# A two-block transformer kernel: query products from whole single-precision weights, embedding weights loaded ahead of the expert rows, values between single query blocks

## What is computed

```python
def _peer(h, w_q, sub_keys_1, sub_keys_2, expert_u, expert_v):
    q = (h @ w_q).reshape(B, S, PEER_HEADS, PEER_DKEY)
    s1 = jnp.einsum('bshd,nd->bshn', q[..., :half], sub_keys_1)
    s2 = jnp.einsum('bshd,nd->bshn', q[..., half:], sub_keys_2)
    v1, i1 = lax.top_k(s1, PEER_TOPK)
    v2, i2 = lax.top_k(s2, PEER_TOPK)
    cand = (v1[..., :, None] + v2[..., None, :])
    best, ci = lax.top_k(cand, PEER_TOPK)
    expert_idx = ia * PEER_NKEYS + ib
    gates = jax.nn.softmax(best, axis=-1)
    a = gelu(einsum('td,thkd->thk', hx, u)) * gx
    return einsum('thk,thkd->td', a, v)
```

## Time and profile before

| | us |
|---|---|
| median of 3 runs | 1351.69 (1349.7 to 1352.07) |
| the profiled execution | 1353.7 |
| its span, first to last instruction | 1352.0 |
| TensorE busy | 1215.2 (90%) |
| VectorE busy | 1059.7 (78%) |
| ScalarE busy | 616.0 (46%) |
| POOL busy | 290.1 (21%) |

### The profile page before, as it was taken

How to read it: one execution, slowest core, us unless ns; L and a number is a source line. 1 busy time by engine, 2 the same in 40 slices (tenths; PEclk the granted TensorE clock), 3 DMA queues, 4 the chain that set the end, 5 groups by cost and what they waited for, 6 DMA issues and landing times. The chain is left out here.

```text
span 1352.0 us, 19494 instructions
## 1 busy us (share of the span) xinstructions
PE 1215.2 (90%) x6952; PEld 908.0 (67%) x6952; DVE 1059.7 (78%) x2161; ACT 616.0 (46%) x1265; POOL 290.1 (21%) x280
## 2 busy tenths in 40 slices
PE   7999999999989877778877777787899999999998
PEld 5999999999743333324332232333699999999998
DVE  7898678887879777777766777777699978898666
ACT  4666555656333333332433333233563265554445
POOL 1010000002545544344444434443000000000000
PEclk9999999999999999999999999999999999999999
DMA  9966446665999999999999999999853545454461
GB/s 388 384 225 249 187 158 235 245 234 234 375 422 426 427 428 428 427 427 427 427 427 427 427 428 428 428 427 428 341 187 126 187 137 183 180 187 173 174 236 43
DMA packets 55488, 416.64 MB, mean 308 GB/s; under 512 B 6113, under 2 KB 6753, under 8 KB 9202
## 3 DMA queue, kind: packets, MB, share of 16 engines
q0 software_dynamic: 37152, 268.45, 47.2%
q1 hardware_dynamic: 17792, 146.51, 29.3%
q10 hardware_dynamic: 466, 0.63, 0.1%
HBM read 414.52 MB, written 1.05 MB: 307 GB/s over the span
## 5 line engine op out<-in xcount | busy, mean ns | idle before, releaser
L1109 PE MATMUL ps<-arena 128*128 128x512 f32 x512 | 234.6, 603 | 57.0 <-ACT arena L1613 57.0
L1109 PE MATMUL ps<-ring,arena 128*128 128x512 f32 x440 | 214.1, 637 | 47.1 <-ACT arena L1613 47.1
L2377 DVE CUSTOM_DVE_ANT_0 arena<-arena 128x1024 f32<-128x1024 f32 x128 | 151.7, 1223 | 99.0 <-DMA arena<-in_experts,rowid 96.3
L1109 PEld LDWEIGHTS ps<-arena 128*128 128x128 f32 x512 | 92.7, 189 | 193.9 <-ACT arena L1613 98.0
L659 POOL DMA_INDIRECT arena<-in_experts,rowid x128 | 128.7, 1005 | 351.7 <-DVE rowid L2304 191.0
L1109 PEld LDWEIGHTS ps<-ring,arena 128*128 128x128 f32 x440 | 86.1, 202 | 170.4 <-issue 92.6
L772 PE MATMUL ps<-h_hi,w_lo 128*128 128x256 f32 x700 | 194.9, 278 | 0.0
L1606 ACT ACTIVATE arena<-arena 128x2 f32<-128x2 f32 x126 | 25.6, 203 | 369.1 <-DVE arena L2377 368.9
L770 PE MATMUL ps<-h_hi,w_hi 128*128 128x256 f32 x672 | 189.0, 281 | 3.0 <-DVE w_lo L1959 2.4
L771 PE MATMUL ps<-h_lo,w_hi 128*128 128x256 f32 x672 | 187.2, 279 | 0.0
L2377 DVE CUSTOM_DVE_ANT_0 ring<-ring,arena 128x1024 f32<-128x1024 f32 x112 | 133.3, 1222 | 35.4 <-DMA ring<-in_experts,rowid 26.5
(11 more groups left out here) (424 smaller groups left out, 2558.4 us busy)
## 6 DMA issues: line engine op xcount, KB each, us to landing
ring<-in_early_w SPq DMA_DIRECT2D x43, 1024.0 KB, 5.0
arena<-in_ada_w SPq DMA_DIRECT2D x24, 1024.0 KB, 8.1
arena<-in_up_w SPq DMA_DIRECT2D x11, 2048.0 KB, 7.8
arena<-in_z_w SPq DMA_DIRECT2D x8, 2048.0 KB, 7.9
arena<-in_down_w SPq DMA_DIRECT2D x8, 1408.0 KB, 6.1
arena<-in_o_w SPq DMA_DIRECT2D x2, 2048.0 KB, 8.1
arena<-in_early_w SPq DMA_DIRECT2D x3, 1024.0 KB, 7.6
arena<-in_experts,rowid POOLq DMA_INDIRECT x128
```

The source lines that it names most:

```text
L1109: mm = pe.matmul(BK[4 + 2 * t + b], diag[:, j, :], rows[j][:, D + b * 512:D + (b + 1) * 512], start=first and j == 0, stop=last and j == ( ...
L2377: v.tensor_tensor_reduce(out=u, in0=u, in1=h2tok[:, t, :], scale=1.0, scalar=0.0, op0=ALU.mult, op1=ALU.add, accum_out=dots[:, even, j:j + ...
```

## The change

- `pq` joins `WHOLE`: query products take the chunk as loaded, and the input `x2` whole, 8 matmuls to a block. `part`, `rest`, `lo_of_x2` for them go. `low_halves` corrects a count.
- Each query chunk has one place; the ring places of rows 9 to 15 are dealt out anew. The last six chunks are loaded in the order `PQ_ORDER`, each after a product of the `wo` stage at the latest.
- `ple_w` moves to memory that `x2_hi` had; the embedding loads follow the query chunks without a wait.
- POOL: six rows at once, more after block 5, and pairs 0 to 5 of step 1 before rows 14 and 15 of step 0.
- TensorE: a value pair of step 0 behind nearly every query block.
- On ScalarE and VectorE the work of heads is reordered accordingly (dots 5 and 6 ahead of scores, weights of pairs 5 to 7 earlier).

```diff
-WHOLE = ("iq", "yb", "ya")
+WHOLE = ("iq", "pq", "yb", "ya")
 PARTED = [n for n, c in enumerate(CHUNKS) if c[0][0] not in WHOLE]
 PARTED_EARLY = len([key for key in EARLY if key[0] not in WHOLE])
 PQ = CHUNK_AT[("pq", 0)]
 BB = CHUNK_AT[("bb", 0)]
-PARTED[PARTED.index(BB):PARTED.index(PQ) + 2] = [BB, PQ, BB + 1, PQ + 1, *range(BB + 2, PQ)]
 PG = CHUNK_AT[("pg", 0)]
 
 
-PQ_HOME = {PQ: ("row", 5, 6, None, None), PQ + 1: ("row", 7, 8, None, None), PQ + 2: ("row", 2, 3, None, None),
-           PQ + 3: ("ring", 0, 5, PQ - 4, PQ - 3), PQ + 4: ("ring", 1, 6, PQ - 3, PQ - 2),
-           PQ + 5: ("ring", 2, 4, PQ - 2, PQ - 1), PQ + 6: ("ring", 3, 5, PQ - 1, PQ + 3),
-           PQ + 7: ("ring", 0, 1, PQ + 3, PQ + 4)}
+PQ_HOME = {PQ: ("row", 8, None), PQ + 1: ("row", 7, None), PQ + 2: ("row", 6, None), PQ + 3: ("ring", 5, PQ - 3),
+           PQ + 4: ("ring", 2, PQ - 2), PQ + 5: ("ring", 6, PQ - 2), PQ + 6: ("ring", 0, PQ - 4),
+           PQ + 7: ("ring", 1, PQ - 3)}
+PQ_ORDER = [PQ + 2, PQ + 6, PQ + 3, PQ + 7, PQ + 4, PQ + 5]
...
-            x2_lo = over.enter_context(nc.sbuf_tensor("x2_lo", [P, KD, T + 2], F32R))
+            x2 = over.enter_context(nc.sbuf_tensor("x2", [P, KD, T + 2], F32))
...
-        in_ring = (6, 2, 4, 3, 5, 0, 1)
+        in_ring = (5, 3, 4, 2, 6, 0, 1)
...
-        ple_w, pleT = pacc, negdist[:, :, :]
+        ple_w, pleT = again(a_hT - 2 * D, NT, D), negdist[:, :, :]
...
+        def query_chunk(c):
+            where, at_home, _ = PQ_HOME[c]
+            return pq_raw[where][:, at_home, :]
...
-                    where, _, _, before, _ = PQ_HOME[n]
-                    if n < PQ + 2:
+                    before = PQ_HOME[n][2]
+                    if before is None:
 
                         sp.wait_ge(S("dsa_cp"), AH)
                         sp.wait_ge(S("ada_dot"), 2 * ADA_HALVES)
-                    elif where == "row":
-
-                        sp.wait_ge(S("taken_V"), taken_by("V", BLOCK_AT[("bb", 7)]))
                     else:
                         sp.wait_ge(S("product"), last_product(before) + 1)
                     if n >= PQ + 4:
 
-                        sp.wait_ge(S("w_hi"), split_count(n - 4))
-                    sp.dma_start(parts(n)[0], w[name][at_w // HALF, :, 0:kt * nn]).then_inc(arrival(n)[0], 16)
+                        sp.wait_ge(*arrival(n - 4))
+                    sp.dma_start(query_chunk(n), w[name][at_w // HALF]).then_inc(arrival(n)[0], 16)
...
-            for n in [*range(2, BB + 1), PQ, PQ + 1, *range(BB + 1, PQ), *range(PQ + 2, FIRST_C)]:
+            for n in [*range(2, BB + 1), PQ, PQ + 1, *range(BB + 1, PQ), *PQ_ORDER]:
...
-            sp.wait_ge(S("product"), BLOCK_AT[("pq", 15)] + 1)
-            sp.wait_ge(S("scores"), N_HEAD)
             sp.dma_start(ple_w.rearrange("p a b -> p (a b)"), w["pl_w"][0]).then_inc(S("p_in"), 16)
             sp.dma_start(pleT, w["ple_t"].rearrange("(k p) t -> p k t", p=P)).then_inc(S("p_in"), 16)
...
-                for j in (0, 1, 4, 5):
+                for j in range(6):
                     gather(j, 0)
                 pool.wait_ge(S("product"), BLOCK_AT[("pq", 5)] + 1)
-                for j in (2, 3, 6, 7):
+                for j in (6, 7, 10, 11):
+                    gather(j, 0)
+                pool.wait_ge(S("h2tok"), 4)
+                pool.wait_ge(S("product"), BLOCK_AT[("pq", 7)] + 1)
+                for j in (8, 9):
                     gather(j, 0)
                 pool.wait_ge(S("rows_ready"), 2)
-                pair(1, 1, 0)
-                pair(1, 1, 1)
-                pool.wait_ge(S("h2tok"), 4)
-                gather(8, 0)
-                pool.wait_ge(S("product"), BLOCK_AT[("pq", 9)] + 1)
-                gather(9, 0)
-                pair(1, 1, 2)
-                pair(1, 1, 3)
-                for p in (5, 6, 7):
-                    pool.wait_ge(S("product"), BLOCK_AT[("pq", 2 * p + 1)] + 1)
-                    for j in (2 * p, 2 * p + 1):
-                        gather(j, 0)
+                for p in range(4):
+                    pair(1, 1, p)
+                pool.wait_ge(S("product"), BLOCK_AT[("pq", 11)] + 1)
+                for j in (12, 13):
+                    gather(j, 0)
+                pair(1, 1, 4)
+                pair(1, 1, 5)
+                pool.wait_ge(S("product"), BLOCK_AT[("pq", 15)] + 1)
+                for j in (14, 15):
+                    gather(j, 0)
 
             def head(g, even, last=False, done=0):
...
-            abreast("pq", 2, x2_hi, x2_lo, "n2", n=T + 2)
+            first = [begin(("pq", b)) for b in range(2)]
+            for k in range(KD):
+                pe.wait_ge(S("x_hi"), halves("n2", k))
+                for b in range(2):
+                    mm = pe.matmul(first[b][0][:, 0:T + 2], first[b][1][:, k, b * P:(b + 1) * P], x2[:, k, :],
+                                   start=k == 0, stop=k == KD - 1, skip_group_check=True)
+                    if k == KD - 1:
+                        mm.then_inc(S("product"), 1)
             norm2_sums()
...
             def query(b):
-                product_parted(("pq", b), x2_hi, x2_lo, n=T + 2)
+                bank, whole = begin(("pq", b))
+                c0 = column(("pq", b))
+                for k in range(KD):
+                    mm = pe.matmul(bank[:, 0:T + 2], whole[:, k, c0:c0 + P], x2[:, k, :], start=k == 0, stop=k == KD - 1)
+                mm.then_inc(S("product"), 1)
...
             values(0)
             head_scores(3)
             query(8)
+            values(1)
             query(9)
-            values(1)
             values(2)
             query(10)
             head_scores(4)
             values(3)
             query(11)
+            values(4)
             query(12)
             head_scores(5)
+            values(5)
             query(13)
             query(14)
             head_scores(6)
             query(15)
-            values(4)
+            values(6)
             head_scores(7)
-            for p in range(5, PAIRS):
-                values(p)
+            values(7)
             with pe.Fori(1, EH - 1, 1) as g:
...
-                if k in (0, 2, 5):
+                if k == 0:
                     part()
                 act.wait_ge(S("taken_V"), taken_by("V", BLOCK_AT[("wo", k)]))
-                act.activation(x2_hi[:, k, 0:T], xT[:, k, :], ACT.Copy, scale=mod[:, k:k + 1]).then_inc(S("x_hi"), 1)
+                act.activation(x2[:, k, 0:T], xT[:, k, :], ACT.Copy, scale=mod[:, k:k + 1]).then_inc(S("x_hi"), 1)
...
-            def lo_of_x2(k):
-
-                v.wait_ge(S("x_hi"), halves("n2", k))
-                if k == 0:
-                    v.tensor_tensor(x2_lo[:, :, T:T + 2],
-                                    adaT[:, 24:32].rearrange("p (a b) -> p a b", b=1).broadcast_to([P, KD, 2]),
-                                    x2_hi[:, :, T:T + 2].bitcast(F32), ALU.subtract)
-                stt(x2_lo[:, k, 0:T], xT[:, k, :], mod[:, k:k + 1], x2_hi[:, k, 0:T].bitcast(F32), ALU.mult, ALU.subtract
-                    ).then_inc(S("x_lo"), 1)
-
             rest()
             for b in range(8):
-                if b in (2, 4):
+                if b == 2:
                     rest()
                 link(stt(xT[:, b, :], arrived(("wo", b))[:, 0:T], adaT[:, 16 + b:17 + b], xT[:, b, :], ALU.mult, ALU.add),
                      "taken_V")
-                if b:
-                    if b < KD - 1:
-                        lo_of_x2(b - 1)
-                    if b == KD - 2:
-                        lo_of_x2(b)
                 if b >= 2 and b < KD - 1:
                     add_to_first("n2", b - 1, hT)
                 if b == KD - 2:
                     add_to_first("n2", b, hT)
-            lo_of_x2(KD - 1)
-            rest()
```

More of the change, by code:

```diff
@@ L200, in halves, with low_halves @@
     return sum(n for _, n in HALVES[:names.index(stage)]) + k + 1
+def low_halves(stage, k=0):
+    names = [name for name, _ in HALVES]
+    return halves(stage, k) - (KD if names.index(stage) > names.index("n2") else 0)
 def norm_count(tag):
@@ L404, in two_blocks @@
         pq_raw = {"row": again(a_raw, 9, HALF), "ring": again(a_ring, RAW + 3, HALF)}
-        pq_r = {"row": alias("pq_row", a_raw, 9, HALF), "ring": alias("pq_ring", a_ring, RAW + 3, HALF)}
         W = KD * 512
@@ L454, in parts @@
             n = CHUNKS[c][2] * CHUNKS[c][5]
-            if c in PQ_HOME:
-                where, lo, hi, _, _ = PQ_HOME[c]
-                return pq_raw[where][:, lo, 0:n], pq_r[where][:, hi, 0:n], pq_r[where][:, lo, 0:n]
             if c < FIRST_C:
@@ L592, in _ @@
                 if key == ("gk", 0):
-                    sp.wait_ge(S("x_lo"), halves("n1", KD - 1))
+                    sp.wait_ge(S("x_lo"), low_halves("n1", KD - 1))
                     sp.dma_start(wuk, w["wuk_t"]).then_inc(S("dsa_in"), 16)
@@ L713, in _ @@
             first_rows()
-            head(1, 1, done=4)
+            head(1, 1, done=6)
             head(2, 0)
@@ L782, in abreast @@
                 for k in range(KD):
```

(44 more changed lines are left out.)

12 lines of the change are left out of this document (5 added, 7 removed).

## The result

The kernel before took 1351.22 us (median of 6 runs, 1349.70 to 1353.23), the changed one **1359.67 us** (6 runs, 1359.12 to 1362.65): ratio 1.0065, 95% interval 1.0055 to 1.0075, 8.45 us slower. The forecast was 1360.8 us, slower with a chance of 0.74. The profiled execution after took 1360.37 us, with a span of 1358.6 us.

What follows compares the result with a forecast made beforehand. The DMA fetch of expert rows at 427 GB/s was taken to bound the kernel; +1.2 - 4.0 - 5.5 + 7.3 + 10.1 = +9.1 us took the median from 1351.69 to 1360.8 us, with an 8-in-10 range of 1349 to 1367.

Steps and rivals of the forecast that it cites:

- First products: First two query blocks: 6.96 instead of 5.76 us at 3.48 a block, so the rows' flow starts 1.2 us later.
- Splits removed: Row fetch at 346 to 360 us: the 4.0 us hole (305 GB/s) counted as gone, -4.0 us.
- Loads out of the stage: Last query chunk and embedding weights, 2.36 MB, leave the row stage for before 300 us: -5.5 us.
- Block 15 at 389.0: Last query block on TensorE ends at 389.0, 15.0 us later: 8 from dearer products, 7 from two value pairs moved ahead.
- First hole: Row stream runs out at 384.6 and flows again at 391.9, behind rows 14 and 15's wait for block 15: 7.3 us.
- Second hole: Row stream stops at 401.7 until 411.8, as the next gather needs value pair 7: 10.1 us.
- The flow is closed again: After the second hole pairs follow every 3.5 us on TensorE against 4.9 on the DMA, so no further loss.
- Sum: All terms for the end of the row stage: +1.2 - 4.0 - 5.5 + 7.3 + 10.1 = +9.1 us.
- What follows the stage takes 399 us and isn't touched: Work from the row stage's end to the span's end stays 399 us, so the stage's shift is the time's change.
- Both holes shut: Rival: block 15 ends by 381.7, rows behind cover the second hole, -8.3 us, 1343.4; chance 0.17.
- Only the second shut: Rival: chain from rows 14 and 15 to value pair 7 is fast enough, -1.0 us, 1350.7; chance 0.09.
- Four full passes: Rival: a whole product costs four present passes, 3.92 us a block, 7.0 us later at block 15, 1367.8; chance 0.08.

Runs made afterwards that it cites:

- experiment 5: Kernel before, splits kept, rows 2 and 3 swapping places with 6 and 7, six rows gathered at once, row 8 ahead of the next head's first pairs: 1348.45 us, ratio 0.9975.
- experiment 4: Kernel before with its embedding weights (1.05 MB) loaded twice at their old place behind block 15: 1353.57 us, ratio 1.0023.
- experiment 3: Changed kernel with the two embedding loads (1.31 MB) put back behind block 15 and the last scores: 1361.09 us, 1.0087 of the kernel before.
- experiment 2: Changed kernel with only 6 of 8 matmul steps in query blocks 2 to 15: 1353.94 us, 1.0033 of the kernel before.
- experiment 6: Changed kernel, last query chunk in the embedding weights' buffer, those weights behind block 15, rows 14 and 15 after block 13 ahead of pairs 4 and 5: 1357.35 us.
- experiment 1: Changed kernel with first-head value pairs 4 to 6 again behind block 15, rows 14 and 15 gathered ahead of the next head's pairs 4 and 5: 1355.09 us.
- experiment 8: Changed kernel with 19 unread matmuls on TensorE between the last scores and value pair 7: 1359.10 us, 1.0057 of the kernel before.

## Why the prediction was right

- **First products, +1.2 us.** Three blocks after the first pair take (320.58 - 310.12) / 3 = 3.49 us; 3.48 was said. The first gather is at 318.08 (318.2 said). In the rates the slower start costs 1.1 us: 0.4 in 318 to 320 (29 GB/s instead of 115), 0.6 in 320 to 322 (287 instead of 418), and a little behind.
- **Splits removed, -4.0 us.** The amount is right, the dip is gone. The reason was half wrong: "POOL is held until the split is done, so part of the 4.0 us hole is this". Experiment 5 keeps the splits and the long gathers and loses the dip. What decides is the stock of rows ahead of a wait, which the prediction gave as its second reason (ten rows asked for at once or after block 5); a split can have cost time only behind that wait, when the stock was out, and how much is open. The page of the Trainium skill that it cited, "SBUF — State Buffer", section "SBUF: two separate sides", says that GpSimd is locked out of the shared port pair during some VectorE instructions and can't write descriptors then. The 3.05 us gathers beside splits agree; that the lock must cost time doesn't follow, as experiment 5 shows.
- **Loads out of the stage, -5.5 us.** The bytes did leave: chunk PQ + 7 and the weights are issued by 296.4. The price of a byte fits where the stream is full (experiment 4: 2.3 us by the medians for 2.5 worked out). In the changed kernel it isn't a gain that could be lost again (experiment 3).
- **Block 15 at 389.0**: 389.35. TensorE's records show no wait before the last scores, and its order held to the block.
- **First hole 7.3 us**: 5.2 in 386 to 394. The missing part lies ahead of it: 1.1 us in 380 to 384 and 1.0 in 360 to 370, where the changed kernel moves 383 GB/s. The prediction counted 26 rows as one unbroken stock, but pair 3 of the second head was asked for only at 363.33 and pair 5 at 378.51, each after the value pair of its number, when the rows asked for before had nearly run out. Together 7.3.
- **Second hole 10.1 us**: 9.6. The dots start at 399.00 (399.2 said), the pair at 402.86 (403.1). The pair takes 6.38 instead of the 5.40 taken from the earlier trace rows, and the next gather is at 410.04 (409.3 said). The length of the idle time doesn't set this: the pair took 5.24 us after 9.29 (experiment 2), 5.50 after 8.65 (experiment 3) and 6.17 after 5.11 (experiment 6). What differs is when the clock came back: it was at 0.50 until 408, nearly the pair's end, in the changed kernel, but only to 398 in experiment 2, where the pair ran from 395.32. So carrying over one pair's 5.40 was a rough guess, 1.0 us short. "The flow is closed again" behind it was too good by the 1.3 us of 414 to 420.
- **Sum.** +9.2 at the landing, +9.1 said; the medians differ by 8.45. That the landing fits to 0.1 us is partly luck: by the rates the terms are +1.1 - 4.0 - 5.5 + 7.3 + 9.6 + 1.3 = +9.8. "What follows the stage takes 399 us and isn't touched" holds for the work, but the profiled execution took 399.2 us there before and 396.5 after. The windows show a part of why, of before (first) and after:

```profile
1160.00:1170.00 10.00, 9.90 (x73) 9.91 (x73) 9.18 (x15) 4.25 (x5) 0.00 (x0) 0.83 0.46 188
```

```profile
1169.00:1179.00 10.00, 10.00 (x91) 10.00 (x90) 9.18 (x13) 5.30 (x5) 0.00 (x0) 1.00 0.45 185
```

Ten microseconds at 0.83 cost 1.7 by estimate, if TensorE sets the pace there. Some 200 us behind the landing the clock falls for a moment in the profiled executions of before and of experiments 1 and 8 (tails of 399.2, 398.9 and 398.8 us), and not in the other seven (396.5 to 398.8). Those seven differ by 2.2 us among themselves, so this fall isn't the whole of it; the rest is open. So the single executions are compared by their landings above. What decides whether it falls there wasn't tried.
- **The rivals.** Both holes shut: this asked for block 15 by 381.7, and with block 15 at 381.1 (experiment 2) only the first shuts; that the rows behind would cover the second was its mistake. Only the second shut: not seen either; where the second shut (experiment 1), the first grew. Four full passes at the present price: refuted, 3.49 us a block. How many passes a whole product makes inside no row shows, only that it doesn't cost four of the present ones. The rule of four passes (the Trainium skill, page "FP8 and Floating Point Precision", section "TensorE Precision Notes") gives 3.92 us with the pass of the earlier trace rows, an estimate; the measurement decides. This case's 1367.8 lies just outside the range that was said to take in most of it.

## What to carry to other kernels

Where one in-order queue feeds the bound resource, write down for each of its waits how much work is in stock ahead of it, and compare that with the time until the wait ends. An edit that frees an engine or bytes doesn't help if it moves the event that this queue waits for; here two swapped pairs of places, with one row moved ahead of a wait, gave 3.2 us, while a change that took out sixteen splits and moved 2.36 MB out of the stage lost 8.45. The last piece of one phase shouldn't lie in a place that the next phase's queue asks for ahead of work that could already go.

## What the runs showed of the hardware

- A gather on POOL takes 3.05 us beside a VectorE split instead of 0.94, and still costs no time while rows are in stock (experiment 5).
- After an idle of 8.58 us TensorE's clock was at its lower level (1.2 GHz) and eight matmuls took 6.38 us; after one of 5.11 us in experiment 6 6.17, after one of 9.29 us in experiment 2 5.24; with unread work instead 3.70. Idle time of TensorE can thus be paid again in the work behind it, and how much hangs on when the clock comes back, not on the length of the idle time.
- Whole single-precision products of 258 columns cost 3.49 us for eight matmuls, 1.19 times the 2.94 of three passes of split ones.
